# An encoder block's token mixer: the triangular inverse kept on its own chunk's lanes, one triangle merged and transposed by VectorE

## The chip, the cores and the metric

The kernel runs on one core of a Trainium2 chip. A core has a matrix engine (TensorE, "PE" in the profile, its weight loads "PEld"), VectorE ("DVE"), ScalarE ("ACT"), GpSimd ("POOL") and SyncE ("SP"), which issues most DMAs. The engines run their own instruction queues in order and meet at semaphores. The metric is the device time of one execution in microseconds. The kernel before took 3065.03 us, the median of three runs (3062.26 to 3070.91).

## The reference

One layer of a streaming encoder, 2048 tokens, width 1024, float32:

1. Token mixing: RMSNorm, one input projection, an RWKV-7 group (8 heads of 64) beside a gated spatial group, one output projection.
2. RMSNorm and cross-attention (4 heads) into 256 memory tokens.
3. RMSNorm and a SwiGLU feed-forward layer, then a last RMSNorm.

The change lies in the RWKV-7 group. Per head the reference runs this recurrence over the tokens:

```python
sa = jnp.einsum('bhvk,bhk->bhv', S, -kk_t)
S = (S * w_t[:, :, None, :]
     + sa[..., None] * (kk_t * a_t)[:, :, None, :]
     + v_t[..., None] * k_t[:, :, None, :])
y = jnp.einsum('bhvk,bhk->bhv', S, r_t)
```

The kernel computes it in chunks of 64 tokens. Within a chunk the steps depend on each other through a strictly triangular 64x64 matrix of scores, so each head and chunk needs the inverse of a unit triangular matrix.

## The kernel before

The kernel has three stages: input projections (to about 612 us of the profiled span), the mixer (about 612 to 1140 us), and the output projection, attention and feed-forward layer (the rest, which is dense matrix products). The change touches the mixer alone.

**Groups and units.** The mixer takes 16 groups of 128 tokens (`GROUPS`, `L`). A group has 8 heads, named by `m` (0 to 3) and `e` (0, 1), and two chunks of 64 tokens, `a` (0, 1): sixteen units. A head's channels lie on 64 partitions, `lane(e)`; a chunk's tokens lie on 64 partitions, `lane(a)`.

**Quarters of the array.** All matmuls of the inverse and of the state are 64x64: operands on 64 partitions, a result on 64 partitions. Each therefore uses one quarter of the array, named here by the half its operands lie on and the half its result goes to. (0 to 0) and (1 to 1) are the two diagonal quarters. A float32 matmul stands in the trace as two records.

**The inverse.** It grows by levels: blocks of 1 are joined to 2 (the "first" step), then b = 2, 4, 8, 16, 32 (`LEVELS`) are joined to 2b. At each level:

- `cross` multiplies the scores with the left blocks of the inverse (to PSUM);
- ScalarE's `evac_x` copies the product to `xm`;
- `merge` multiplies with the right blocks;
- VectorE's `take_level` puts the result into the inverse under a mask (`copy_predicated`).

The left factor must be had transposed, so `tu` holds each unit twice, as T and as its transpose U. `merge` computes both sides with two matmuls for each unit (L1911 for T, L1913 for U; at the last level U alone). U of a unit lies on the lanes `up(e, a)`, which is `a` for e = 1 and the other chunk's for e = 0. `first_pairs` makes blocks of 2 with 32 small matmuls (L1882, L1884). Every level goes in two halves, g = 0 and 1, of eight units: PE, ACT and DVE each do one half while another does the other. The inverse is used by `solve` (L1968).

**The order.** Three pipelines run beside each other in one body: state work of group k, the inverse of group k + 1 ("behind"), and the preparation of group k + 2 ("ahead"). Each engine's `body` writes its order out by hand. On PE (L1995 on): from_values, state_out 0, state_in 0, scores b, solve 0, scores k, state_add 0, chunk_out 0, first_pairs, state_out 1, state_in 1, cross 0, solve 1, merge 0, state_add 1, cross 1, chunk_out 1, loras, merge 1, key_norms, variance, turn_gate, cross 2, turn k, merge 2, turn b, cross 3, turn_v, merge 3, bonus_sums, key_scales, scale_back, cross 4, lora_g, mix_gate, merge 4. On DVE: right_sides 0, scores b (two `take`), next_state 0, first (2), right_sides 1, scores k (2), level 0, next_state 1, gate_sigmoid, level 1, sum_decays (sig, cum, k_mix), gate_stats, level 2, reciprocals, deviation, level 3, bonuses, keys_normed, normalised, queries, mixed, level 4, decayed. On ACT: identities, solved 0, loras_in, gate_in, evac 0, solved 1, evac 1, outputs, lora_tanh, evac 2, k_tok, roots, deviation, evac 3, b_tok, v_tok, exps, evac 4, gates.

Of the kernel before, what the change touches and what calls it, by code (L numbers as in the profile page):

```python
# [13 lines left out]
P = 128  # L14
# [56 lines left out]
def hybrid_block_kernel(nc, xT, memT, gains, weights, shift_mu, w_lora, a_lora, g_lora, head_cols,  # L71
                        kk_rows, lnx_rows, kk_cols, rk_spread, w_spatialT, b_spatial, sgu_ln, consts, cen,
                        head_mean, scan_reset, block_masks, tri_masks, half_ident, tri_wide, outT):
    with ExitStack() as ctx:
# [164 lines left out]
        tu = [rw(f"tu{i}", [P, 2, 2, 2, 2, C]) for i in range(2)]  # L239
# [43 lines left out]
        for n in ("const_in in_first in0 in1 in2 in3 xr_in0 xr_in1 sqa_done ws_zero const_ready mixers_done w_raw0 w_raw1 w_hi_done w_lo_done job_done job_out act_in sq_done sumsq_done "  # L283
# [7 lines left out]
                  "id_done sc_b sc_k sc_1 ev_b ev_k x_ps x_ev tu_ps tu_ev rhs_ps rhs_ev sa_ps sa_ev h_ps h_add h_new "  # L291
# [161 lines left out]
        def up(e, a):  # L453

            return a ^ 1 ^ e

        def both(t, g, b):

            first = t[:, g]
            return bass.AP(first.tensor, first.offset, [[16 * C, P], [4 * C + b, 2], [2 * b, 2 * C // b], [1, b]])  # L460

        def rights(t, g, b):
            return t[:, g, 1].rearrange("p e m (n two b) -> p (e m n) two b", two=2, b=b)[:, :, 1, :]
# [622 lines left out]
        def _(act):  # L1086
# [107 lines left out]
            def identities(n, par):  # L1194
                if n >= 2:
                    act.wait_ge(S["sa_ps"], 2 * n - 2)
                act.activation(tu[par][:].rearrange("p g u e m t -> p (g u e m) t"), half_id[:].unsqueeze(1).to_broadcast([P, 4 * HP, C]),
                               ACT.Copy).then_inc(S["id_done"], 1)
# [433 lines left out]
        def _(pe):  # L1632
# [221 lines left out]
            def scores(n, par, src, need, bank, done):  # L1854
# [3 lines left out]
                if n:  # L1858
                    pe.wait_ge(S["tu_ev"], 12 * n)
                elif bank:  # L1860
                    pe.wait_ge(S["job_out"], 2 * Q_TAIL)
# [1400 lines left out]
```

## Time and profile before

| what | value |
|---|---|
| runs, median (lowest to highest) | 3065.03 us (3062.26 to 3070.91) |
| profiled execution: span | 3061.7 us |
| share of the span that PE is busy | 97% |
| granted TensorE clock, mean over the span | 0.98 of full |
| DVE, ACT, POOL busy | 53%, 33%, 47% |
| the mixer's 15 stretches from one `from_values` to the next | 498.54 us |
| PE busy, mean granted clock in the fastest and slowest of them | 28.22 of 30.25 us at 1.00; 32.57 of 35.22 us at 0.85 |

The span runs from the first to the last instruction that the profiler recorded; the execution that was profiled has no other time of its own, and what lies around the span is seen only as the 3.3 us between it and the median of the runs. Busy time is the union of an engine's records. A PE record lasts about 0.22 us though the next one can start after 0.01 to 0.03 us, so the length of a step is read from start to start.

### The profile page before, as it was taken

The page shows a single profiled execution, that of the slowest core. Times are in us where ns is not written, and L with a number is a line of the kernel's source. Part 1 is how long each engine was busy: PE and PEld are TensorE (multiplying, and loading weights), DVE is VectorE, ACT ScalarE, POOL GpSimd, SP SyncE. Part 2 cuts the span into 40 slices and gives each one's busy share as a digit, 9 for nine tenths or more (in the row PEclk, how much of TensorE's full clock was granted, in tenths as well). Part 3 has the DMA queues.
Part 4 walks back from the last instruction along what each step waited for, and adds up shares of the span by engine and source line. Part 5 has one row for each costly group of instructions (what it writes and reads, how often), then busy time and mean ns, then how long its engine had stood idle before and what let it go on. Part 6 is the DMA issues. An engine that isn't in the chain of part 4 may idle for free.

```text
span 3061.7 us, 62501 instructions
## 1 busy us (share of the span) xinstructions
PE 2955.4 (97%) x26858; PEld 2523.8 (82%) x26858; DVE 1613.3 (53%) x2010; ACT 1001.8 (33%) x1692; POOL 1432.3 (47%) x993
## 2 busy tenths in 40 slices
PE   8999999989998989999999999999999999999998
PEld 7888888788888878998788888787898788888887
DVE  6332643365666653234866664545232876665452
ACT  4123211233443442233433332222232433332222
POOL 4555454333443445437544442446625654443344
PEclk9999999988998999999999999999999999999999
DMA  4433454321112222111223326454111123335642
GB/s 167 165 102 111 159 161 157 123 59 43 43 49 67 68 60 93 42 42 42 110 110 138 138 111 254 173 198 158 42 48 49 69 110 125 138 125 217 231 152 85
DMA packets 176012, 347.25 MB, mean 113 GB/s; under 512 B 47232, under 2 KB 104576, under 8 KB 170112
## 3 DMA queue, kind: packets, MB, share of 16 engines
q1 hardware_dynamic: 175744, 343.35, 32.5%
q8 instruction: 208, 3.41, 0.5%
q14 instruction: 60, 0.49, 0.1%
HBM read 240.53 MB, written 102.76 MB: 112 GB/s over the span
## 4 chain that ended last, share of the span: by engine, by line
PE 70%; DVE 6%; issue 2%; DMA 2%; ACT 1%; POOL 1%; SPq 0%; DVEq 0%; ACTq 0%; POOLq 0%
PE ps L2201 28%; PE ps L1641 19%; PE ps L2153 6%; PE ps L1747 2%; PE ps L1911 2%; PE ps L1913 2%; PE ps L1895 2%; PE ps L1865 1%; DMA w_raw<-in_weights 1%; DVE tu L2481 1%; DMA hidden<-hid 1%; PE ps L1992 1%; PE ps L1796 1%; PE ps L1819 1%; PE ps L1851 1%
## 5 line engine op out<-in xcount | busy, mean ns | idle before, releaser
L803 POOL TENSOR_TENSOR w_lo<-w_raw,w_hi 128x512 fp32r<-128x512 f32 x256 | 383.1, 1519 | 503.8 <-ACT w_hi L1093 500.0
L1641 PE MATMUL ps<-a_hi,w_hi 128*128 128x512 f32 x1140 | 446.3, 391 | 16.1 <-DVE a_lo L2381 9.6
L1641 PE MATMUL ps<-a_lo,w_hi 128*128 128x512 f32 x1140 | 444.4, 390 | 0.0
L1093 ACT ACTIVATE w_hi<-w_raw 128x512 fp32r<-128x512 f32 x252 | 144.8, 623 | 656.9 <-PE ps L1641 509.8
L1641 PE MATMUL ps<-a_hi,w_lo 128*128 128x512 f32 x1140 | 351.5, 390 | 0.0
L2201 PE MATMUL ps<-a_hi,w_hi 128*128 128x512 f32 x800 | 314.8, 393 | 10.3 <-ACT u_t L1462 4.9
L2201 PE MATMUL ps<-a_lo,w_hi 128*128 128x512 f32 x800 | 313.2, 391 | 0.0
L2201 PE MATMUL ps<-a_hi,w_lo 128*128 128x512 f32 x800 | 312.9, 391 | 0.0
L1641 PEld LDWEIGHTS ps<-a_hi,w_hi 128*128 128x128 f32 x1140 | 214.5, 188 | 62.9 <-DVE a_lo L2381 9.6
L1641 PEld LDWEIGHTS ps<-a_hi,w_lo 128*128 128x128 f32 x1140 | 214.3, 188 | 44.9
L1641 PEld LDWEIGHTS ps<-a_lo,w_hi 128*128 128x128 f32 x1140 | 214.5, 188 | 44.1 <-issue 0.2
L1020 POOL TENSOR_TENSOR w_lo<-w_raw,w_hi 128x512 fp32r<-128x512 f32 x100 | 139.8, 1398 | 182.6 <-ACT w_hi L1453 182.6
L1020 POOL TENSOR_TENSOR w_lo<-s,w_hi 128x512 fp32r<-128x512 f32 x100 | 143.8, 1438 | 169.5 <-ACT w_hi L1453 169.5
L2736 DVE TENSOR_TENSOR x<-ps,x 128x1024 f32 (+1 forms) x63 | 76.6, 1221 | 268.3 <-PE ps L1641 255.6
L2389 DVE TENSOR_TENSOR z_ext<-ps,rstd 128x1024 f32<-128x1024 f32 x44 | 53.9, 1225 | 305.0 <-PE ps L1641 304.5
L1641 PE MATMUL ps<-b_hi,w_hi 128*128 128x512 f32 x512 | 202.7, 396 | 3.7 <-DVE x L2736 3.7
L1641 PE MATMUL ps<-b_lo,w_hi 128*128 128x512 f32 x512 | 201.4, 393 | 0.0
L1020 POOL TENSOR_TENSOR xw_lo<-s,xw_hi 128x512 fp32r<-128x512 f32 x100 | 145.1, 1455 | 109.8 <-ACT xw_hi L1453 109.8
L2201 PE MATMUL ps<-t_hi,xw_hi 128*128 128x512 f32 x496 | 193.1, 389 | 0.2
L2201 PE MATMUL ps<-t_hi,xw_lo 128*128 128x512 f32 x496 | 193.0, 389 | 0.0
L2201 PE MATMUL ps<-t_lo,xw_hi 128*128 128x512 f32 x496 | 193.0, 389 | 0.0
L2201 PEld LDWEIGHTS ps<-a_hi,w_hi 128*128 128x128 f32 x800 | 151.2, 189 | 46.1 <-ACT u_t L1462 6.6
(369 smaller groups left out, 6658.3 us busy)
## 6 DMA issues: line engine op xcount, KB each, us to landing
w_raw<-in_weights SPq DMA_DIRECT2D x228, 512.0 KB, 4.0
hidden<-hid SPq DMA_DIRECT2D x44, 1024.0 KB, 3.9
zT<-z_out SPq DMA_DIRECT2D x44, 512.0 KB, 3.8
a_hi<-hidden SPq DMA_DIRECT2D x44, 512.0 KB, 8.2
a_lo<-hidden SPq DMA_DIRECT2D x44, 512.0 KB, 9.1
w_raw<-kvw SPq DMA_DIRECT2D x32, 512.0 KB, 3.2
suv<-zT SPq DMA_DIRECT2D x16, 512.0 KB, 5.0
x<-in_xT SPq DMA_DIRECT2D x16, 512.0 KB, 6.1
```

The lines of the kernel that those rows point to most:

```text
L803: pool.tensor_tensor(low_t[:, u, part, :], w_raw[:, u, part, :], high[:, u, part, :].bitcast(F32), ALU.subtract).then_inc(S["w_lo_done"], 1)
L1020: pool.tensor_tensor(operand(o, p)[1], operand_raw[o], operand(o, p)[0].bitcast(F32), ALU.subtract).then_inc(S["sw_lo"], 1)
L1093: act.activation(split_into(pair)[0][:, u, part, :], w_raw[:, u, part, :], ACT.Copy).then_inc(S["w_hi_done"], 1)
L1641: mm = pe.matmul(to[:, nb, 0:w], wt[:, u, k, :], r[:, k, nb * w:(nb + 1) * w], start=(k == 0 and r is hi_in and wt is w_hi), stop=(k == kn ...
L1747: mm = pe.matmul(cols(bank, m), lhs[:, m * P:(m + 1) * P], rhs[:, (m // 2) * C:(m // 2) * C + L], start=True, stop=True)
L1895: mm = pe.matmul(unit(h, 2 * g * (lv > 0) + e, 2 * L + g * C * (lv == 0) + mh * 32, 32), atrb[par][lane(a), e, 2 * mh + g, 0, :], t_u, sta ...
L1911: pe.matmul(unit(a, *t_at, 32), u_u, x_u.rearrange("p (n two b) -> p n two b", two=2, b=b)[:, :, 0, :], start=True, stop=True)
L1913: mm = pe.matmul(unit(h, 2 * g + 1, (e + 1) * C + mh * 32, 32), x_u, u_u.rearrange("p (n two b) -> p n two b", two=2, b=b)[:, :, 1, :], st ...
L2153: mm = pe.matmul(to, st[:, k, at:at + P], wt[:, 0:2, k, :], start=(k == 0 and n == 0 and t % 2 == 0), stop=(k == KT - 1 and n == 2), skip_ ...
L2201: mm = pe.matmul(to, wt[:, k, :], r[:, k, :], start=(k == 0 and n == 0 and not more), stop=(k == HT - 1 and n == 2), skip_group_check=True)
L2389: dve.tensor_tensor(z_ext[:, u, 1:TB + 1], flat(src), rstd[:], ALU.mult).then_inc(S["job_out"], 1)
L2736: dve.tensor_tensor(at_k(x, k), flat(slot(beside + u)).unsqueeze(1), at_k(x, k), ALU.add).then_inc(S["job_out"], 1)
```

## The change

The inverse of a unit stays on its own chunk's lanes, once (`inv`). Only one triangle is merged on PE. The transposed operand that `cross` needs is made by a VectorE instruction, `transpose`, over all sixteen units (512 columns), which transposes each 32x32 block into `inv_t`. `first_pairs` is gone: DVE takes the odd columns out of the scores themselves. Each level is one step for all sixteen units, on PE, ACT and DVE.

```diff
-        tu = [rw(f"tu{i}", [P, 2, 2, 2, 2, C]) for i in range(2)]
+        inv = [rw(f"inv{i}", [P, 2, HP, C]) for i in range(2)]
+        inv_t = rw("inv_t", [P, 2, HP, C])
 ...
-                if lv == 0:
-                    if n == 0:
-                        act.wait_ge(S["late_zero"], 1)
-                    act.wait_ge(S["x_ps"], 10 * n + 2)
-                    act.activation(xm[:].rearrange("p e g m (n two b) -> p e (g m n) two b", two=2, b=b)[:, :, :, 0, :],
-                                   ps[:, 0:2, 2 * L:2 * L + 2 * C].rearrange("p e (n b) -> p e n b", b=b), ACT.Copy).then_inc(S["x_ev"], 2)
-                    return
-                for g in range(2):
-                    act.wait_ge(S["x_ps"], 10 * n + 2 * lv + g + 1)
-                    act.activation(xm[:, :, g].rearrange("p e m (n two b) -> p e (m n) two b", two=2, b=b)[:, :, :, 0, :],
-                                   ps[:, 2 * g:2 * g + 2, 2 * L:2 * L + C].rearrange("p e (n b) -> p e n b", b=b), ACT.Copy
-                                   ).then_inc(S["x_ev"], 1)
+                if n == 0 and lv == 0:
+                    act.wait_ge(S["late_zero"], 1)
+                act.wait_ge(S["x_ps"], 5 * n + lv + 1)
+                act.activation(xm[:].rearrange("p e g m (n two b) -> p e (g m n) two b", two=2, b=b)[:, :, :, 0, :],
+                               ps[:, 0:2, 2 * L:2 * L + 2 * C].rearrange("p e (n b) -> p e n b", b=b), ACT.Copy).then_inc(S["x_ev"], 1)
 ...
-            def by_tile(g):
-
-                return [(mh, e, a, up(e, a)) for mh in range(2) for e in range(2) for a in range(2)]
-
-            def first_pairs(n, par):
-
-                pe.wait_ge(S["ev_b"], 2 * n + 2)
-                for g in range(2):
-                    for mh in range(2):
-                        for a in range(2):
-                            for e in range(2):
-                                m, at = 2 * mh + g, 2 * L + g * C + mh * 32
-                                q_u, b_u = qr[par][lane(e), 0, m, a, :], bt[lane(e), m, a * C:(a + 1) * C]
-                                pe.matmul(unit(a, e, at, 32), q_u,
-                                          b_u.rearrange("p (n two) -> p n two", two=2)[:, :, 0], start=True, stop=True)
-                                mm = pe.matmul(unit(up(e, a), e, L + at, 32), b_u,
-                                               q_u.rearrange("p (n two) -> p n two", two=2)[:, :, 1], start=True, stop=True)
-                mm.then_inc(S["sc_1"], 1)
+            def by_tile():
+
+                return [(m, e, a) for m in range(HP) for e in range(2) for a in range(2)]
 
             def cross(n, par, lv):
 
                 b = LEVELS[lv]
-                for g in range(2):
-                    pe.wait_ge(S["tu_ev"], 12 * n + 2 * lv + (g + 1 if lv else 2))
-                    for mh, e, a, h in by_tile(g):
-                        t_u = tu[par][lane(a), g, 0, e, mh, :].rearrange("p (n two b) -> p n two b", two=2, b=b)[:, :, 0, :]
-                        mm = pe.matmul(unit(h, 2 * g * (lv > 0) + e, 2 * L + g * C * (lv == 0) + mh * 32, 32),
-                                       atrb[par][lane(a), e, 2 * mh + g, 0, :], t_u, start=True, stop=True)
-                    mm.then_inc(S["x_ps"], 1)
+                if lv == 0:
+                    pe.wait_ge(S["ev_b"], 2 * n + 2)
+                pe.wait_ge(S["inv_tr"], 5 * n + lv + 1)
+                for m, e, a in by_tile():
+                    t_u = inv_t[lane(a), e, m, :].rearrange("p (n two b) -> p n two b", two=2, b=b)[:, :, 0, :]
+                    mm = pe.matmul(unit(a, e, 2 * L + m * 32, 32), atrb[par][lane(a), e, m, 0, :], t_u, start=True, stop=True)
+                mm.then_inc(S["x_ps"], 1)
 
             def merge(n, par, lv):
 
                 b = LEVELS[lv]
-                last = lv == len(LEVELS) - 1
-                for g in range(2):
-                    pe.wait_ge(S["x_ev"], 10 * n + 2 * lv + g + 1)
-                    if lv == 0:
-                        pe.wait_ge(S["ev_k"], 2 * n + 2)
-                    for mh, e, a, h in by_tile(g):
-                        x_u, u_u = xm[lane(h), e, g, mh, :], tu[par][lane(h), g, 1, e, mh, :]
-                        if not last:
-                            t_at = (2 * g + 1, mh * 32) if e else (2 * g, BANK - C + mh * 32)
-                            pe.matmul(unit(a, *t_at, 32), u_u,
-                                      x_u.rearrange("p (n two b) -> p n two b", two=2, b=b)[:, :, 0, :], start=True, stop=True)
-                        mm = pe.matmul(unit(h, 2 * g + 1, (e + 1) * C + mh * 32, 32), x_u,
-                                       u_u.rearrange("p (n two b) -> p n two b", two=2, b=b)[:, :, 1, :], start=True, stop=True)
-                    mm.then_inc(S["tu_ps"], 1)
 ...
                 for m, e, a in by_pair(j):
-                    mm = pe.matmul(unit(up(e, a), 4 + e, j * L + (m % 2) * C), qr[par][lane(e), 0, m, a, :], h_st[lane(e), j, m, :],
+                    mm = pe.matmul(unit(a, 4 + e, j * L + (m % 2) * C), qr[par][lane(e), 0, m, a, :], h_st[lane(e), j, m, :],
 ...
                 for m, e, a in by_pair(j):
-                    mm = pe.matmul(unit(a, 6 + e, (2 + j) * L + (m % 2) * C), tu[par][lane(up(e, a)), m % 2, 1, e, m // 2, :],
-                                   rhs_t[lane(up(e, a)), e, m % 2, :], start=False, stop=True, skip_group_check=True)
+                    mm = pe.matmul(unit(a, 6 + e, (2 + j) * L + (m % 2) * C), inv[par][lane(a), e, m, :],
 ...
+            def turned(n, par, lv):
+
+                dve.wait_ge(S["tu_ev"], 6 * n + lv + 1)
+                dve.transpose(inv_t[:].rearrange("p e m t -> p (e m) t"), inv[par][:].rearrange("p e m t -> p (e m) t")).then_inc(S["inv_tr"], 1)
 
             def take_first(n, par):
-                dve.wait_ge(S["sc_1"], n + 1)
+                dve.wait_ge(S["sc_b"], n + 1)
                 dve.wait_ge(S["id_done"], n + 1)
-                first = ps[:, 0:2, 2 * L:].rearrange("p e (u g x) -> p u g e x", u=2, g=2)
-                for g in range(2):
-                    base = tu[par][:, g]
-                    out = bass.AP(base.tensor, base.offset, [[16 * C, P], [4 * C + 1, 2], [2 * C, 2], [2, C]])
-                    take(out, low[:, 0].rearrange("p u (e x) -> p u e x", e=2), first[:, :, g], "tu_ev")
+                odd_cols = inv[par][:].rearrange("p e m (x two) -> p e m x two", two=2)[:, :, :, :, 1]
+                mask = low[:, 0, 1].rearrange("p (m x) -> p m x", m=HP).unsqueeze(1).to_broadcast([P, 2, HP, C // 2])
+                take(odd_cols, mask, ps[:, 0:2, :].rearrange("p e (m w x two) -> p e m w x two", w=2, x=C // 2, two=2)[:, :, :, 0, :, 1], "tu_ev")
+                turned(n, par, 0)
 
             def take_level(n, par, lv):
                 b = LEVELS[lv]
-                for g in range(2):
-                    dve.wait_ge(S["tu_ps"], 10 * n + 2 * lv + g + 1)
-                    new = ps[:, 2 * g:2 * g + 2, :].rearrange("p b t -> p (b t)")[:, BANK - C:BANK + 3 * C]
-                    if lv < len(LEVELS) - 1:
-                        take(both(tu[par], g, b), blocks(low[:, lv + 1], b), blocks(new.rearrange("p (u x) -> p u x", u=2), b), "tu_ev")
-                    else:
-                        take(rights(tu[par], g, b), low[:, lv + 1, 1].rearrange("p (n b) -> p n b", b=b),
-                             new[:, 2 * C:].rearrange("p (n b) -> p n b", b=b), "tu_ev")
+                dve.wait_ge(S["tu_ps"], 5 * n + lv + 1)
+                mask = low[:, lv + 1, 1].rearrange("p (x b) -> p x b", b=b).unsqueeze(1).to_broadcast([P, 2, HP * C // (2 * b), b])
+                take(rights(inv[par], b).rearrange("p (e x) b -> p e x b", e=2), mask,
+                     ps[:, 0:2, 0:HP * C // 2].rearrange("p e (x b) -> p e x b", b=b), "tu_ev")
+                if lv + 1 < len(LEVELS):
+                    turned(n, par, lv + 1)
 ...
                                        0.0, ALU.mult, ALU.add).then_inc(S["cum_done"], 1)
+
+            def mixing(n):
+                dve.wait_ge(S["sig_done"], n + 1)
```

`from_values` writes to `unit(a, ...)` in place of `unit(up(e, a), ...)` in the same way. The orders written out by hand become:

- PE: ..., scores k, state_add 0, **cross 0**, chunk_out 0, state_out 1, state_in 1, **merge 0**, solve 1, **cross 1**, state_add 1, **merge 1**, chunk_out 1, loras, **cross 2**, key_norms, variance, **merge 2**, turn_gate, turn k, **cross 3**, turn b, **merge 3**, turn_v, **cross 4**, bonus_sums, key_scales, **merge 4**, scale_back, lora_g, mix_gate.
- DVE: right_sides 0, **first + transpose**, scores b, next_state 0, scores k, right_sides 1, **level 0 + transpose**, next_state 1, **level 1 + transpose**, gate_sigmoid, sum_decays (sig, cum), **level 2 + transpose**, mixing (k_mix, four instructions), gate_stats, reciprocals, deviation, **level 3 + transpose**, bonuses, keys_normed, **level 4**, normalised, queries, mixed, decayed.
- ACT: as before, with one evacuation of 256 columns in each level and 512 in place of 1024 columns in `identities`.

## Rows read from the trace of the kernel before

**Rows 1.** The page: busy time by engine, and the chain by engine.
```profile
PE 2955.4 (97%) x26858; PEld 2523.8 (82%) x26858; DVE 1613.3 (53%) x2010; ACT 1001.8 (33%) x1692; POOL 1432.3 (47%) x993
...
PE 70%; DVE 6%; issue 2%; DMA 2%; ACT 1%; POOL 1%; SPq 0%; DVEq 0%; ACTq 0%; POOLq 0%
```

**Rows 2.** Windows by body: stretch, its length, busy us by engine, clock, DMA.
```profile
671.77:706.99 35.22, 32.57 (x940) 29.80 (x936) 21.65 (x44) 14.06 (x30) 14.72 (x14) 0.85 0.18 46
...
981.73:1013.08 31.35, 28.24 (x940) 25.55 (x936) 21.09 (x44) 14.20 (x30) 14.46 (x12) 1.00 0.27 69
...
1045.60:1075.85 30.25, 28.22 (x940) 25.63 (x937) 21.52 (x44) 14.02 (x30) 14.45 (x12) 1.00 0.29 74
...
sum 498.54, PE 450.56 PEld 411.27 DVE 313.90 ACT 206.54 POOL 209.78; mean PE 30.04 PEld 27.42 DVE 20.93 ACT 13.77 POOL 13.99
```

**Rows 3.** Groups by line, PE, fifteen bodies: records, busy, mean ns, idle before, releasers.
```profile
L1911 PE MATMUL ps<-xm,tu 64*64 64x32 f32 x1920 | 98.2, 232 | 2.3 <-DVE qkrm L2481 2.0
L1895 PE MATMUL ps<-tu,atrb 64*64 64x32 f32 x2400 | 63.2, 233 | 13.6 <-DVE tu L2481 8.1 <-issue 4.8
...
L1882 PE MATMUL ps<-bt,qr 64*64 64x32 f32 x480 | 18.5, 219 | 9.1 <-issue 9.1
...
L1992 PE MATMUL ps<-atrb,sa_t 64*64 64x64 f32 x480 | 16.8, 249 | 1.1 <-issue 1.1
```

**Rows 4.** Windows inside one body, cut where the granted clock changes.
```profile
810.85:822.20 11.35, 8.45 (x399) 7.76 (x396) 7.02 (x14) 2.20 (x6) 5.50 (x6) 1.00 0.37 90
822.30:829.00 6.70, 6.55 (x141) 6.19 (x137) 2.29 (x5) 1.64 (x4) 0.00 (x0) 0.50 0.31 85
```

**Rows 5.** Timeline of PE: start us, length us, line, output<-inputs, records.
```profile
1048.11 0.41 PE L1968 MATMUL ps<-rhs_t,tu 64*64 64x64 f32 x16
1048.34 0.41 PE L1974 MATMUL ps<-v_tok,k_tok 64*64 64x64 f32 x16
...
1064.04 0.66 PE L1840 MATMUL ps<-cst,kt 128*128 128x128 f32 x4
...
1066.18 0.66 PE L1840 MATMUL ps<-cst,bt 128*128 128x128 f32 x4
...
1072.40 0.67 PE L1895 MATMUL ps<-tu,atrb 64*64 64x32 f32 x32
1073.00 1.16 PE L1747 MATMUL ps<-gd,gl 128*128 128x128 f32 x8
...
1075.11 0.95 PE L1913 MATMUL ps<-tu,xm 64*64 64x32 f32 x26
1075.85 0.27 PE L1928 MATMUL ps<-v_tok,qkrm 64*64 64x64 f32 x2
```

**Rows 6.** Timeline of DVE, same columns.
```profile
1048.35 1.38 DVE L2481 COPY_PREDICATED atrb<-tri,ps 128x512 f32<-128x512 uint8 x2 [0.65 <-PE ps L1865]
...
1051.85 1.30 DVE L2481 COPY_PREDICATED tu<-low,ps 128x256 f32<-128x256 uint8 x2 [0.60 <-PE ps L1884]
...
1061.69 0.43 DVE L2481 COPY_PREDICATED tu<-low,ps 128x256 f32<-128x256 uint8 x1 [2.90 <-PE ps L1913]
...
1062.74 0.68 DVE L2537 TENSOR_SCALAR sig<-th 128x1024 f32<-128x1024 f32 x1
1063.45 1.23 DVE L2541 TENSOR_TENSOR_SCAN cum<-reset,sig 128x512 f32<-128x512 f32 x1
...
1068.18 0.71 DVE L2568 TENSOR_SCALAR v_hat<-ps,bn 128x512 f32<-128x512 f32 x1
```

**Rows 7.** Timeline of ACT, same columns.
```profile
1048.59 0.38 ACT L1240 ACTIVATE sa_t<-ps 128x256 f32<-128x256 f32 x1 [3.11 <-PE ps L1968]
...
1054.62 0.40 ACT L1174 ACTIVATE xm<-ps 128x256 f32<-128x256 f32 x1 [4.63 <-PE ps L1895]
...
1060.83 1.02 ACT L1204 ACTIVATE th<-ps 128x1024 f32<-128x1024 f32 x1 [1.07 <-PE ps L1747]
...
1067.00 0.36 ACT L1216 ACTIVATE n<-ps,eps 128x128 f32<-128x128 f32 x1
```

More of the change, by code:

```diff
@@ L290, in hybrid_block_kernel @@
                   "lg_ps gate_done bon_ps bon_v bonus_done vtr ktr btr vtc ktc btc "
-                  "id_done sc_b sc_k sc_1 ev_b ev_k x_ps x_ev tu_ps tu_ev rhs_ps rhs_ev sa_ps sa_ev h_ps h_add h_new "
+                  "id_done sc_b sc_k inv_tr ev_b ev_k x_ps x_ev tu_ps tu_ev rhs_ps rhs_ev sa_ps sa_ev h_ps h_add h_new "
                   "qkv_ps y0_ps y_ps yc_cp yc_sq yv_ps yv_rt yv_rc yb_ps yn_done yb_done yo_done y_st met_pe met_dve met_sp").split():
@@ L451, in side, with rights @@
             return j ^ (m // 2)
[L453 to L463, printed above, removed]
+        def rights(t, b):
+            return t[:].rearrange("p e m (n two b) -> p (e m n) two b", two=2, b=b)[:, :, 1, :]
         def bank4(b):
@@ L1917, in from_values @@
+                pe.wait_ge(S["x_ev"], 5 * n + lv + 1)
+                for m, e, a in by_tile():
+                    u_u = inv[par][lane(a), e, m, :].rearrange("p (n two b) -> p n two b", two=2, b=b)[:, :, 1, :]
+                    mm = pe.matmul(unit(a, e, m * 32, 32), xm[lane(a), e, m // 2, m % 2, :], u_u, start=True, stop=True)
+                mm.then_inc(S["tu_ps"], 1)
             def from_values(k, par):
@@ L1927, in from_values @@
                     for m, e, a in by_pair(j):
-                        mm = pe.matmul(unit(up(e, a), 4 + e, j * L + (m % 2) * C), qkrm[par][lane(a), e, m, 0, :], v_tok[par][lane(a), m, e, :],
+                        mm = pe.matmul(unit(a, 4 + e, j * L + (m % 2) * C), qkrm[par][lane(a), e, m, 0, :], v_tok[par][lane(a), m, e, :],
                                        start=(j == 0 and m % 2 == 0), stop=True, skip_group_check=True)
@@ L2009, in body @@
                     state_add(k, par, 0)
+                if behind:
+                    cross(b, q, 0)
+                if state:
                     chunk_out(k, par, 0)
-                if behind:
-                    first_pairs(b, q)
-                if state:
                     state_out(k, par, 1)
@@ L2016, in body @@
                 if behind:
-                    cross(b, q, 0)
+                    merge(b, q, 0)
                 if state:
@@ L2020, in body @@
                 if behind:
-                    merge(b, q, 0)
+                    cross(b, q, 1)
                 if state:
@@ L2024, in body @@
                 if behind:
-                    cross(b, q, 1)
+                    merge(b, q, 1)
                 if state:
@@ L2030, in body @@
                 if behind:
-                    merge(b, q, 1)
+                    cross(b, q, 2)
                 if ahead:
@@ L2035, in body @@
                     variance(k)
+                if behind:
+                    merge(b, q, 2)
                 if ahead:
@@ L2038, in body @@
                 if behind:
-                    cross(b, q, 2)
                     turn(b, kt, "kt_done", 4, ahead, "ktr")
-                    merge(b, q, 2)
+                    cross(b, q, 3)
                     turn(b, bt, "bt_done", 5, ahead, "btr")
-                    cross(b, q, 3)
+                    merge(b, q, 3)
                     turn_v(b, q, ahead, state)
-                    merge(b, q, 3)
+                    cross(b, q, 4)
                     bonus_sums(b, q)
@@ L2048, in body @@
                     key_scales(n)
+                if behind:
+                    merge(b, q, 4)
                 if state:
@@ L2051, in body @@
                 if behind:
-                    cross(b, q, 4)
                     lora_g(b, q)
@@ L2055, in body @@
                     mix_gate(n, state)
-                if behind:
-                    merge(b, q, 4)
             for pair in range(Q_IN1, Q_TAIL):
@@ L2623, in body @@
                 if scores:
+                    take_first(b, q)
                     take_scores(b, atrb[q], 0, "sc_b", "ev_b")
@@ L2636, in body @@
                 if scores:
+                    take_level(b, q, 1)
                     gate_sigmoid(b, q)
-                    take_level(b, q, 1)
                 if ahead:
                     sum_decays(n)
-                    gate_stats(n)
                 if scores:
@@ L2644, in body @@
                 if ahead:
+                    mixing(n)
+                    gate_stats(n)
                     reciprocals(n)
@@ L2652, in body @@
                     keys_normed(n, state)
+                if scores:
+                    take_level(b, q, 4)
                 if state:
@@ L2657, in body @@
                     mixed(n)
-                if scores:
-                    take_level(b, q, 4)
-                if ahead:
                     decayed(n)
@@ L2681, in _ @@
                         sum_decays(0)
+                        mixing(0)
                         gate_stats(0)
```

14 lines of the change are left out of this document (6 added, 8 removed).

## The prediction

> **What bounds the kernel now.** I read the page first. PE is busy for 97% of the span, and the chain that ended last runs 70% on PE, with DVE far behind at 6% [rows 1]. So a change pays only if PE gets through sooner. The change touches the mixer, so the next view is the windows cut by body, from one `from_values` to the next. Fifteen of them last 498.54 us, 33.2 each; PE is busy for 30.0 of that, DVE for 20.9, ACT for 13.8 and POOL for 14.0 [rows 2]. Of the bodies run wholly at full clock (three: 31.35 to 30.25 us) the mean is 31.4. The reader is to see that PE has only about 3 us of idle time in a body. The groups by line say whose it is: eleven groups lose 35.2 us together to "issue", from 9.1 (L1882) down to 1.1 (L1992), with no engine named, 2.3 us a body; `cross` (L1895) loses 8.1 to DVE's `tu` [rows 3]. The last view is the windows inside a body: its sparse part (PE busy for 8.45 of 11.35 us) is followed by 6.7 us at a granted clock of 0.50, which is 1.2 GHz [rows 4]. PE had idled before the fall.
>
> **What a 64x64 step costs PE.** The timeline at full clock gives four. `cross` 4 puts 32 records on all four quarters, 8 on each, and the next step starts 0.60 us later. Merge 4 has 32 records on the two diagonal quarters only, and its first 26 (13 a quarter) span 0.95. `solve`, 16 records on four quarters, gives way after 0.23. Merge 2 fills the time between the transposes of kt and bt, 2.14 us less the 0.58 of the first: 1.56 [rows 5]. One rule fits all: a record holds its quarter for 0.058 us, and the fullest quarter sets the step. Cross 4: 8 x 0.058 = 0.47, plus 0.13 of handing over. The 26 records: 12 x 0.058 + the record's own 0.22 = 0.92 (0.95 read). Solve: 4 x 0.058 = 0.23. Merge 2: 64 records, but T for e = 0 alone leaves the diagonal, so each diagonal quarter holds 24: 1.40 + 0.16.
>
> **The change on PE, per body.** It keeps every unit on its own lanes, so cross, merge, from_values and solve now use the diagonal quarters alone.
> - first_pairs goes: 16 records a quarter, -0.93.
> - Four merges go from 24 to 16 on the fullest quarter: 4 x -0.47 = -1.87. Merge 4 stays at 16.
> - Five crosses go from 8 to 16: 5 x +0.47 = +2.33.
> - Two solves go from 4 to 8: 2 x +0.23 = +0.47. from_values goes from 8 to 16: at most +0.47; today it starts behind merge 4's quarters, so I take half, +0.24.
>
> Sum +0.24 us. 192 records of 940 leave each body and PE gains nothing.
>
> The Trainium skill speaks otherwise in one place: "TensorE: Matmul & The Clock Gate", Part 3 (The mechanism), says that a weight load overlaps matmuls in flight only when the row group differs. By that the new order, which alternates the two row halves, would run as fast as cross today. The trace does not settle it, since merge 4's order is 1, 0, 0, 1, but its 0.95 us is nearer to the quarter rule; the other case is a rival below.
>
> **The change on the chain.** Today the halves g = 0 and 1 cover each other. Afterwards each level is one string: cross, evacuation, merge, take, transpose, cross. Prices: ACT 0.40 for 256 columns (L1174) [rows 7]; DVE's masked copy of 256 columns 0.43, but 1.30 for two where it writes runs of one or two elements (first, level 0), which overlap by 0.1, so about 0.74 for one that is waited for; the score copies 1.38 for two [rows 6]; from PE's last start to a reader 0.30 (solve 1048.34, `sa_t` 1048.59), back to PE 0.05 [rows 5, 7]. DVE `transpose` stands nowhere in the trace. Lower bound 0.40: `sig` does 1024 columns in 0.68, half is 0.34 and a start. Upper bound 1.3: the scan needs 1.23 for 512. `v_hat` needs 0.71 for 512 [rows 6]; I take 0.70, the row of the same size. By the skill's "VectorE: DVE Perf Modes" (The three transpose paths: 311 ns for 128x128 bf16; Specifications: 0.96 GHz) an estimate would be 0.31 + 384/0.96 ns = 0.71.
>
> Walking the new order once at full clock, PE will wait at the places below; where I write 0.1 it is two hand-overs of 0.05.
> 1. Cross 0, for `ev_b`: 0.30 + first 0.74 + transpose 0.70 + two score copies 1.39 = 3.1 after scores b; over it lie solve 0.47, the token products 0.23, scores k 0.88, state_add 0.23. Wait 1.3. Behind it are queued chunk_out 0 and state_out 1, so the state recurrence waits too.
> 2. state_out 1, for chunk_out 0's own end (first_pairs covered it): 0.3.
> 3. Cross 1: 0.30 + 0.74 + 0.70 + 0.1 = 1.8, less solve and products 0.70: 1.1.
> 4. Merge 1: 0.30 + 0.40 + 0.05 less state_add 0.23: 0.5.
> 5. Merge 2: 0.75 less norms and variance 0.56: 0.2 (`lora_tanh`'s 1.02 on ACT [rows 7] is as long as the cross).
> 6. Cross 3: 0.30 + 0.43 + 0.70 + 0.1 less two steps of 0.60: 0.4 (sig and cum, 1.9 on DVE [rows 6], delay level 2 a little).
> 7. Merge 3: evac 3 stands on ACT behind the root of gate_stats, and gate_stats now on DVE behind level 2, its transpose and k_mix. From cross 3's start: 1.0 + 0.6 + 0.15 on DVE, two roots 0.6, evacuation 0.4 = 2.75; over it cross 3 1.06 and turn b 0.60. Wait 1.1.
> 8. Cross 4, behind three reciprocals, v_hat and level 3 with its transpose: 3.7 after the root, less 0.7 + merge 3 1.06 + turn_v 1.10: 0.9.
> 9. Merge 4, behind exps: 0.2.
>
> Together 6.0 us. The k_mix delay of 0.4 us for POOL costs nothing: POOL's string ends before the next body's scores b need it.
>
> **The sum.** The fastest body is 30.25 long, PE idle for 2.0 of it [rows 2], and at each of its five waits a record's end of 0.22 counts as busy though no step needs it: 30.25 - 2.0 - 1.1 = 27.1 of steps. With 31.4 for a body at full clock that leaves 4.3 for waits and issue. Afterwards: 27.1 + 0.24 + 6.0 + issue. Issue idles fall where 64x64 records come thickest, in the first part of a body: 399 in 11.35 us [rows 4]; that part loses first_pairs' 64 and merge 0's 32 and becomes longer. I take 2.3 -> 0.5 (bounds 0 and 2.3). New body 33.8, so +2.4 at equal clock. Fourteen such bodies give +34; the first and last, with parts missing, +2 together (the first has less work to lay over the string, the last has DVE and ACT freed). ACT's identities halves from 1024 columns, off the path. SP's queue and DMAs are untouched. 3061.7 + 36 = 3098 of span; the median of the runs lies 3.3 above the span, so **3101 us**. Nothing outside the mixer moves.
>
> **Rivals.**
> - *Diagonal quarters at row-group speed.* Cross stays at 0.47, merges fall to it: PE work -5.1 us in place of +0.24, of which half turns into longer waits because PE laid that work over the string (body about 30.7 + 0.5). Against 31.4 that is -0.2 a body, 3062; with a 0.4 us transpose -1.0 a body, about 3050, and this is the case that ends faster. It decides at a cross step under 0.7 us. Against it: merge 4's 0.95. Chance 0.15 (0.09 of it faster, 0.06 near no change).
> - *The clock.* PE idles longer and oftener, and today a fall follows the sparse part [rows 4]. Half as much again of the 6.7 us at 1.2 GHz in each body, 3.4, costs up to 1.7: 14 x 1.7 = 24, giving 3125. Against it: bodies as sparse kept 1.00 [rows 2]. Chance 0.25.
> - *A slow transpose.* At 1.3 us, +0.6 at each of five; where it lies open +2.2 a body: 3132. Chance 0.08.
> - *The walk overstates waits.* If in-order idle overlaps the issue idle as it does today, +1.0 a body remains: 3079 (3070 to 3085). Chance 0.12, a third of it within no change.
>
> Forecast as summed: 0.40. Over 0.3% is what a measurement of this kernel can tell from no change, so the bounds are 3056 and 3074. Faster 0.11, same 0.14, slower 0.75. The range 3052 to 3138 leaves out the far end of the first rival and a slow transpose at a low clock.
>
> **What would show it.** Right: L1895 with 32 records takes about 0.95 us from start to next step, merges the same; PE busy in a body unchanged near 28 at full clock though its records fall to 748; PE idle named by `inv_t` and `xm`, 5 to 6 us; "issue" under 1 us. Wrong: cross steps of 0.6; transposes of 0.4 or over 1; PE idle still mostly "issue"; full-clock bodies under 32 us. The forecast fails on its sign if full-clock bodies stay under 31.4.

## The result and the profile after

The changed kernel takes 3097.79 us (median of 4 runs, 3095.98 to 3107.98), the kernel before 3064.24 (median of 4): ratio 1.0099, 95% interval 1.0068 to 1.0131. It is slower, and 3 us under the 3101 forecast. The profiled spans are 3061.7 and 3094.2 us.

The page after: busy time by engine, and the first line of the chain that ended last.
```profile
PE 2952.9 (95%) x23786; PEld 2519.3 (81%) x23786; DVE 1628.2 (53%) x1994; ACT 984.1 (32%) x1628; POOL 1433.3 (46%) x993
...
PE 16%; DMA 2%; DVE 1%; ACT 0%; SPq 0%; issue 0%; POOL 0%; DVEq 0%; ACTq 0%
```
3072 records of PE are gone [rows 1], 192 in each of the sixteen bodies as counted, and PE is busy for only 2.5 us less. The chain is no help here: followed back from the end it now breaks off before it comes to the mixer. So I read windows.

Windows of the kernel after (stretch, length, busy us by engine, granted clock, DMA share, GB/s): two bodies at full clock, and all fifteen.
```profile
1006.27:1040.74 34.47, 28.42 (x743) 25.63 (x741) 23.05 (x41) 13.09 (x27) 14.17 (x12) 1.00 0.24 62
1040.74:1074.20 33.46, 27.95 (x743) 25.41 (x741) 22.14 (x41) 13.05 (x26) 14.52 (x12) 1.00 0.25 64
649.41:1172.52 523.11, 444.47 (x11051) 402.58 (x11049) 328.47 (x601) 190.71 (x381) 208.30 (x173) 0.94 0.19 51
```
A body's window has 743 records in place of 940 (by their starts 740 and 932, which is the 192; a window also counts those that reach into it), but PE is busy for the same 28 us of it [rows 2]. Over the full-clock bodies (three before, seven after, the shorter last body left out) the means are 28.31 busy and 3.07 idle before, 28.30 busy and 5.66 idle after: 31.37 and 33.95 us. The three before are 30.25, 31.36 and 32.52 us long, so their mean is known to about a microsecond only. All that a body became longer is idle time of PE.

Groups by line of PE after, the fifteen bodies (records, busy, mean ns, idle before them, what ended it).
```profile
L1876 PE MATMUL ps<-inv,xm 64*64 64x32 f32 x2400 | 88.5, 225 | 18.9 <-ACT xm L1166 17.2 <-issue 1.6
L1867 PE MATMUL ps<-inv_t,atrb 64*64 64x32 f32 x2400 | 87.5, 224 | 44.3 <-DVE inv_t L2455 31.0 <-DVE atrb L2443 12.9
```
Against [rows 3] the picture has turned round: cross waits 44.3 us in place of 13.6, and "issue" (PE idle though it waits for nothing that the profile shows), which had 36.1 us of 48.0 over all PE groups before, has 4.8 of 78.6 after.

The timeline of PE after, in the body from 1006.27 (start, length, line, output<-inputs, records, idle before and its releaser).
```profile
1027.34 1.12 PE L1867 MATMUL ps<-inv_t,atrb 64*64 64x32 f32 x32 [0.26 <-DVE inv_t L2455]
1028.40 0.66 PE L1826 MATMUL ps<-cst,bt 128*128 128x128 f32 x4
1030.07 1.12 PE L1876 MATMUL ps<-inv,xm 64*64 64x32 f32 x32 [1.02 <-ACT xm L1166]
1031.12 1.16 PE L1837 MATMUL ps<-cent,zin 128*128 128x128 f32 x8
1033.28 1.12 PE L1867 MATMUL ps<-inv_t,atrb 64*64 64x32 f32 x32 [1.00 <-DVE inv_t L2455]
...
1039.71 1.09 PE L1815 MATMUL ps<-ws,v_lnb 128*64 128x128 f32 x16 [0.79 <-DVE y_n L2579]
```
A cross now holds PE for 1.06 us from its start to the next step's (1027.34 to 1028.40), against 0.60 in [rows 5]; a merge for 1.05. In order the rows are cross 3, the turn of bt, merge 3, turn_v, cross 4 and, last, `mix_gate`, which waits for y_n.

The timeline of DVE in the same body.
```profile
1009.96 0.74 DVE L2443 COPY_PREDICATED inv<-low,ps 128x256 f32<-128x256 uint8 x1 [0.89 <-PE ps L1851]
1010.73 0.71 DVE L2455 STREAM_TRANSPOSE inv_t<-inv 128x512 f32<-128x512 f32 x1
1011.37 1.29 DVE L2443 COPY_PREDICATED atrb<-tri,ps 128x512 f32<-128x512 uint8 x2
...
1038.56 0.44 DVE L2443 COPY_PREDICATED inv<-low,ps 128x256 f32<-128x256 uint8 x1
1038.89 0.68 DVE L2579 TENSOR_TENSOR y_n<-y_cen,ps 128x512 f32<-128x512 f32 x1
```
The transpose takes 0.71 us. The last two rows, with the last of PE's above, show what I had not seen coming: y_n stands behind the copy of level 4, and the gate's matmuls on PE wait for it.

### The profile page after: what moved, and what is told of

Same layout as the page of the kernel before. It is cut to its first block and busy times, and to the rows that moved or that the text cites. A ratio compares the mean times of both kernels' runs of the same rounds, so it can differ in the third digit from the quotient of the medians.

```text
span 3094.2 us, 56260 instructions
## 1 busy us (share of the span) xinstructions
PE 2952.9 (95%) x23786; PEld 2519.3 (81%) x23786; DVE 1628.2 (53%) x1994; ACT 984.1 (32%) x1628; POOL 1433.3 (46%) x993
```

## The experiments

**How the times are compared.** Executions of one kernel differ by up to 43 us (the kernel before, 3053.22 to 3096.21), and with them the mean granted clock: the changed kernel took 3086.28 us at 0.985 and 3108.72 at 0.977. Inside each kernel the two lie on a line; over 124 executions of eleven kernels its common slope is 2.24 us (+-0.17) per 0.001 of clock. "At equal clock" below is each kernel's mean brought to 0.980 with it: my working, beside the measured medians. The +- is the 95% interval of that mean from the kernel's own executions; with four of them it is wide. The slopes of single kernels lie between 1.65 and 3.09, and the line takes the clock for something that comes from outside, though part of it is the kernel's own doing (see below). So I read the result beside the trace. The last three columns are means over the full-clock bodies of the trace, without the last body; bodies of one kernel differ by up to 2.3 us, and some kernels have three such bodies or none. The 49 executions of the kernel before were made beside the experiments; the four of the result are not among them.

| kernel | median us (runs) | clock | at equal clock | full-clock body | PE busy in it | idle |
|---|---|---|---|---|---|---|
| before | 3069.6 (49) | 0.980 | 3069.2 +-1.1 | 31.37 | 28.31 | 3.07 |
| after, e5_after_again | 3097.8 (8) | 0.980 | 3099.3 +-1.5 | 33.95 | 28.30 | 5.66 |
| e1_before_diag_cross | 3081.9 (10) | 0.982 | 3088.0 +-1.2 | 33.10 | 30.47 | 2.63 |
| e2_quarters | 3090.3 (10) | 0.975 | 3079.6 +-2.0 | 33.42 | 26.22 | 7.19 |
| e3_no_transpose | 3098.9 (4) | 0.973 | 3080.4 +-7.9 | 33.75 | 28.56 | 5.19 |
| e4_order | 3059.7 (10) | 0.983 | 3068.6 +-2.0 | 31.38 | 28.08 | 3.30 |
| e6_gate_only | 3103.2 (4) | 0.974 | 3086.9 +-5.5 | none | - | - |
| e7_before_fewer_t | 3044.2 (9) | 0.982 | 3048.7 +-2.4 | 30.72 | 26.96 | 3.77 |
| e8_order2, e11 | 3022.7 (9) | 0.987 | 3038.2 +-1.2 | 29.65 | 28.08 | 1.56 |
| e9_fill | 3077.8 (7) | 0.991 | 3104.4 +-1.0 | 34.04 | 29.53 | 4.51 |
| e10_order2_fill | 3017.5 (4) | 0.991 | 3042.7 +-3.7 | 29.69 | 28.07 | 1.62 |

**The quarter rule, in both kernels and both directions.** In the kernel before:
```diff
-  mm = pe.matmul(unit(h, 2 * g * (lv > 0) + e, ...   # cross
+  mm = pe.matmul(unit(a, 2 * g * (lv > 0) + e, ...
```


> The kernel before, with one change: the cross matmuls of the inverse write their results to the lanes that they read from, so that they use the two diagonal quarters of TensorE in place of all four (the products land on other units' lanes than the reference's; counts, sizes and waits are those of before). Quarter rule (each record holds its quarter for 0.058 us, the fullest quarter sets the step): a cross of one half, 32 records, goes from 8 to 16 records a quarter, its step from 0.60 to about 1.05 us; over five levels up to +2.3 us of PE a body, some of it hidden in issue idle that is there today, so +1.4 to +2.3 a body, in sixteen bodies +20 to +36 us: about 3084 to 3100 in all. Rival (only a change of row group matters, diagonal quarters run as fast as four): cross step stays at 0.60, total within 0.3% of before.

In the changed kernel:
```diff
-  mm = pe.matmul(unit(a, e, 2 * L + m * 32, 32), ...   # cross
+  mm = pe.matmul(unit(a ^ 1 ^ e, e, 2 * L + m * 32, 32), ...
```


> The changed kernel, with one thing different: the cross matmuls write to the other chunk's lanes for half of their records, so that all four quarters of TensorE are used (the products land on other units' lanes than the reference's; counts, sizes and waits are the changed kernel's). Quarter rule: the cross step falls from 1.05 to 0.60 us, but the string cross, evacuation, merge, copy, transpose goes on as long as before behind it, so only part of the 5 x 0.45 is gained, about 0.9 us a body and 14 us in all: 3084, between 3075 and 3090. Rival (row groups): no change of the step, 3098.

One full-clock body of each, first e1, then e2 (windows, columns as above), and two steps of e2 (timeline of PE).
```profile
1060.77:1094.42 33.65, 30.49 (x940) 28.02 (x937) 22.80 (x44) 14.16 (x30) 14.41 (x12) 1.00 0.26 66
```
```profile
890.50:924.17 33.67, 26.49 (x742) 23.51 (x740) 22.98 (x41) 13.09 (x27) 14.30 (x14) 1.00 0.22 55
```
```profile
911.09 0.67 PE L1867 MATMUL ps<-inv_t,atrb 64*64 64x32 f32 x32 [0.64 <-DVE inv_t L2455]
913.77 1.12 PE L1876 MATMUL ps<-inv,xm 64*64 64x32 f32 x32 [1.42 <-ACT xm L1166]
```
The same records cost +2.16 us of PE a body on two quarters in place of four, and -2.08 the other way; by the rule it is 2.33. The cross of e2 lasts 0.67 in place of 1.12. The row-group rival would have had both at nothing and is refuted: which quarters a step loads sets its time. The totals say less than the steps: e1 is slower than before by 0.48% (interval 0.13 to 0.82) or 18.8 us at equal clock, a little under the range expected (its median, 3081.85, too). e2 is 19.7 us (+-2.3) below the changed kernel at equal clock, where 14 were expected, but its clock is lower, its median falls by only 7.5 us, to the edge of the range, and its three full-clock bodies are only 0.53 us shorter (0.9 expected). What the quarters are worth in the step is shown, what they are worth in the total lies between 8 and 20 us.

**The transpose.**
```diff
-  pe.wait_ge(S["inv_tr"], 5 * n + lv + 1)
+  pe.wait_ge(S["tu_ev"], 6 * n + lv + 1)      # and cross reads inv; no dve.transpose
```


> The changed kernel without VectorE's five transposes of the merged inverse per body: cross reads the merged inverse itself and waits for the copy that wrote it (so the computation leaves the transposition out). If the string of each level is what PE waits for, the 0.71 us goes from the places where it stands open (cross 0, 1, 3, 4, partly refilled by other waits): about 1.4 us a body, 20 us in all, 3078, between 3068 and 3085. Rival (PE's own work is the bound and the transposes lie beside it): within 0.3% of the changed kernel, 3098. If the transposes alone were the loss, it would return to 3064 or below.

At equal clock 18.9 us go, but with four executions that is +-8, and the trace shows less: its execution had the clock of the changed kernel's (0.982) and a span 12.7 us shorter, 9.2 of them in the fifteen bodies (513.9 against 523.1, with 58.4 and 58.7 us at half clock). The median does not move (3098.92), outside the range expected; the executions ran at clocks from 0.967 to 0.982. So the transposes cost something like 10 to 20 us here, and no run fixes it closer. PE's idle time in the fifteen bodies falls from 78.6 to 68.0 only: waits for the inverse go from 31.2 to 13.9 and for `atrb` from 12.9 to 3.4, but `xm` (17.3 to 22.2) and issue (4.8 to 11.9) come up in their place. Even with no transpose at all the kernel stays about 11 us (+-8) above the one before at equal clock: it is one part of the string, not the cause by itself.

**The order of the work.** Nothing is left out in any of these. The order of e4:
```diff
-ACT  k_tok, roots (with root_gate), deviation, evac_x 3
+ACT  k_tok, roots, evac_x 3, root_gate, deviation
-DVE  deviation, take 3, bonuses, keys_normed, take 4, normalised
+DVE  take 3, deviation, bonuses, keys_normed, normalised, take 4
-PE   cross 0, chunk_out 0 ... cross 1, state_add 1, merge 1, chunk_out 1 ... merge 4, scale_back
+PE   chunk_out 0, cross 0 ... state_add 1, cross 1, chunk_out 1, merge 1 ... scale_back, merge 4
```


> The changed kernel with the same work in another order, nothing left out. ACT: the evacuation of cross 3 goes ahead of the roots of gate_stats. VectorE: the take of level 3 goes ahead of gate_stats' deviation part, that of level 4 behind normalised (mix_gate waits 0.58 us a body for it today). PE: chunk_out 0 ahead of cross 0, state_add 1 ahead of cross 1, chunk_out 1 ahead of merge 1, scale_back ahead of merge 4. If the loss of the change is waits in the string and not PE's work, 2.5 to 3.4 us of them go from a body: full-clock bodies of about 31 in place of 34.0, 3055 to 3065 in all, level with the kernel before or a little below. Rival (the waits only move, since the string of five levels is as long as what can be laid over it): at most 1 us a body, 3083 to 3098. A third: what was hidden by them becomes late elsewhere (the state recurrence or the gates), over 3098.

And one part of it alone:
```diff
-DVE  take 4, normalised
+DVE  normalised, take 4
-PE   merge 4, scale_back
+PE   scale_back, merge 4
```


> The changed kernel, nothing left out, with one part of the reordering alone: scale_back ahead of merge 4 on PE, normalised ahead of the take of level 4 on VectorE. It takes away the wait of mix_gate for y_n, 8.7 us in fifteen bodies, that the prediction did not list. If each wait counts by itself: 0.4 to 0.6 us a body, 6 to 9 us in all at an equal clock, 3087 to 3091. Rival (the time comes back at the next body's scores b or at level 4, since the same string follows): no change within 3 us.

Groups by line of e4, the fifteen bodies; they answer to the two rows of after above.
```profile
L1882 PE MATMUL ps<-inv,xm 64*64 64x32 f32 x2400 | 89.9, 226 | 9.2 <-ACT xm L1166 5.4 <-issue 3.7
L1873 PE MATMUL ps<-inv_t,atrb 64*64 64x32 f32 x2400 | 88.7, 225 | 26.1 <-DVE inv_t L2461 17.1 <-DVE atrb L2449 6.4 <-issue 0.9
```
The waits of the two groups fall from 63.2 to 35.3 us, a full-clock body from 33.95 to 31.38 with about the same PE work (28.30 and 28.08). That is the whole loss of the change, undone by order alone: 3059.66 us, ratio 0.9971 to the kernel before (0.9929 to 1.0013, not told apart from it), and at equal clock 0.6 us (+-2.2) from it. e6 takes away the one wait that the prediction missed. It goes (8.7 us for y_n, now none; idle in all 78.6 to 65.1), and at equal clock 12.4 us go (+-5), which holds the 6 to 9 expected; but the median is 3103.22, over the range. The clock was at 0.974.

**The other side of the change by itself**: the kernel before with fewer T merges.
```diff
-  if not last:
+  if lv == 0:
       pe.matmul(unit(a, *t_at, 32), u_u, ...
```


> The kernel before with the merge matmuls of T left out in levels 1 to 3 (only the U side is merged there; level 0 still merges both; VectorE's copies and all waits stay, so the T that cross reads is old). 96 of 940 records a body go, all from the diagonal quarters. Quarter rule and issue supply together: each of three merges goes from 24 to 16 records on its fullest quarter, 3 x 0.47 = 1.4 us a body, and some of the 2.3 us of issue idle goes as well; 21 to 33 us in all at an equal clock, 3031 to 3045. Rival (VectorE's takes or PE's other steps would be late in their place): under 10 us.

PE busy falls by 1.35 us a body (1.4 expected), the ratio is 0.9922 (0.9901 to 0.9942), at equal clock -20.5 us (+-2.5), just under what was expected: issue idle falls from 36.1 to 29.4, but waits for `tu` rise from 8.8 to 15.4 and for `bt` from 0.5 to 5.6. So the removal of T was worth having; what the change paid for it, on PE, was five crosses on two quarters.

**The order taken further.**
```diff
-PE   turn kt, cross 3, turn bt, merge 3, turn_v, cross 4, bonus_sums, key_scales
+PE   turn kt, turn bt, cross 3, turn_v, merge 3, bonus_sums, cross 4, key_scales
+PE   cross 0: the 16 records of e = 0 once their copy is done, then those of e = 1
-ACT  evac_x 2, k_tok, roots, evac_x 3, root_gate, deviation
+ACT  evac_x 2, roots, deviation, k_tok, evac_x 3, root_gate
-DVE  mixing, gate_stats, key reciprocal, v_hat, take 3 ... queries, mixed, decayed
+DVE  gate_stats, mixing, v_hat, take 3, key reciprocal ... decayed, mixed, queries
```


> The order of the run e4_order, nothing left out, and these as well. PE: the turn of bt ahead of cross 3, turn_v ahead of merge 3, bonus_sums ahead of cross 4; cross 0 begins with the units of e = 0 once their scores are copied. ACT: the roots of the key norms and of the deviation ahead of the copy of k_tok. VectorE: gate_stats ahead of mixing; the reciprocal of the key norms behind the take of level 3; decayed, mixed, queries in place of queries, mixed, decayed. Of the 3.1 us of waits in a full-clock body of e4_order (scores b 0.49, cross 0 0.57, sa_t 0.26, cross 1 0.13, cross 3 0.47, merge 3 0.37, cross 4 0.84) about 2.0 go: full-clock bodies of 29.4 in place of 31.4, 30 us less in all, 3025 to 3040, and faster than both kernels. Rival (the string of five levels, three times 1.5 and twice 0.75 us between the steps, is then itself what the body lasts, or VectorE with its 23 us busy becomes late): 3045 to 3060.

Windows of e8: one body, the last body, and all fifteen.
```profile
971.04:1001.09 30.05, 28.21 (x743) 25.86 (x741) 23.11 (x42) 13.17 (x27) 14.20 (x12) 1.00 0.28 71
1060.20:1100.47 40.27, 34.56 (x690) 31.76 (x689) 15.63 (x28) 8.42 (x18) 9.72 (x8) 0.66 0.16 54
645.01:1100.47 455.46, 427.35 (x11050) 392.18 (x11049) 339.82 (x601) 192.77 (x382) 207.34 (x176) 0.97 0.23 59
```
3022.66 us, ratio 0.9843 (0.9813 to 0.9873): faster than both. Fourteen bodies last 29.2 to 30.2 us (29.4 expected) with PE idle for 1.6. The rival, a string that no order can cover, is refuted. One thing was off, in its favour: its clock is 0.987, so that it is a little better than the range (at equal clock, 3038.2, it lies inside). And its last body, with less work in it, runs for 27 of its 40.3 us at half clock, which is what the mean of 0.66 in its row says; the stretch of 30.7 us that the text on e10 names goes on behind the body. What such an order would give the kernel before, which idles for 3.07 us a body, I have not tried.

**What brings the clock down.** Kernels e2, e3 and e6 gained 12 to 20 us at equal clock and gave most or all of it back in a lower clock (for e2 and e6 clear of the spread; e3's four executions are too few for that); e8 gained both ways. In the trace before, all 11 falls in the fifteen bodies begin 7.6 to 14.6 us into a body, in the sparse part [rows 4]. In the two traces of the changed kernel 9 of 16 begin at 22.5 to 25.5, a place where none began before. One of them (windows of the kernel after):
```profile
968.71:991.40 22.69, 19.08 (x590) 17.54 (x588) 15.95 (x32) 8.06 (x18) 5.27 (x5) 1.00 0.35 91
991.40:1005.05 13.65, 13.62 (x136) 12.53 (x136) 5.47 (x10) 3.87 (x7) 8.20 (x7) 0.50 0.00 0
```
The granted clock is 1.00 in the first row and 0.50, which is 1.2 GHz, in the second. PE is busy through the whole of the slow stretch; it had idled ahead of it, for 0.47 us at cross 3 and 0.97 at merge 3. All nine begin like this, in the last 0.1 us of merge 3's wait or up to 1.5 us behind it, and ahead of the wait of cross 4. So I filled the wait of merge 3, and that of cross 4 with it:
```diff
+  def fill(n):                              # ahead of merge 3, and ahead of cross 4
+      pe.wait_ge(S["ev_k"], 2 * n + 2)
+      for i in range(6):
+          pe.transpose(cols(2 + i % 2, i // 2), ident, ident)
```


> The changed kernel again, unchanged, on the chip that runs the three others of this set, so that they have it beside them and so that its time can be read against the granted clock of many executions. 3092 to 3106; at a mean granted clock of 0.982 about 3096.

> The changed kernel, nothing left out, with idle transposes of the identity put on PE ahead of merge 3 and ahead of cross 4: six each, 0.7 us each, into two banks that nothing reads then. They lie in waits of 1.02 and 1.00 us, so the steps start when they did. In the traces of the changed kernel 9 of 16 falls of the granted clock begin at 22.5 to 25.5 us of a body, behind these waits. If the falls there come from PE's idle time: hardly any fall begins there, the mean granted clock goes from 0.980 to 0.986 or more, and the time to 3080 to 3090, while at an equal clock it stays. Rival (the falls have another cause, or more work on PE brings more of them): falls at the same place, clock within 0.002 of the changed kernel's, 3096 to 3106.

Windows of e9, the fifteen bodies.
```profile
644.30:1155.35 511.05, 443.01 (x11230) 401.86 (x11229) 335.90 (x601) 191.21 (x382) 208.41 (x175) 0.99 0.20 52
```
No fall begins at that place, there are two in all (at 13.2 and 18.4), and half-clock time in the fifteen bodies goes from 58.7 and 92.2 us in the two traces of the changed kernel to 10.2. Work that computes nothing makes the kernel 20 us faster: 3077.81 (3075.35 to 3083.47) against 3086.28 to 3108.72, a little more than expected. A full-clock body is no shorter (34.04), and at equal clock the kernel is 5 us slower (+-1.6), where I had expected no change: so the gain is the clock alone, less those 5 us. Another chip is not behind it, since the kernel before kept its clock there (mean of ten executions 0.980). That the falls at this place go when the waits before them are filled is shown. Elsewhere the changed kernel had 7 falls in thirty bodies and e9 has 2 in fifteen, too few to tell. The changed kernel's own repetition (e5) was spread wider than expected, 3086.28 to 3108.72. Why e2 (with more idle time than the changed kernel), e3 and e6 (with less) had a lower clock than it, is not shown: I can't name from the rows what tells a body that falls from one that doesn't.

And the same in the further order, in the first and the last body only:
```diff
+  if not state:  fill(4, 6)    # ahead of cross 0; 4 ahead of merge 0, 8 ahead of cross 1, 5 ahead of merge 1
+  if not ahead:  fill(2, 14)   # in place of loras; 6 in place of turn_gate
```


> The order of e8_order2, nothing left out, with idle transposes of the identity on PE in the first and the last body alone, where parts of the work are missing (23 in the first, 0.12 us each, in the waits of levels 0 and 1; 20 in the last in place of loras and turn_gate). In the trace of e8_order2 the granted clock is at half for 30.7 us of the last body, which lasts 40.3 us in place of 29.5, and the first lasts 36.0. If idle time lets the clock fall there: the last body under 36 us, the first under 34, together 5 to 12 us less, 3011 to 3018. Rival (fill delays the string where the wait is shorter than it, and the clock falls all the same): 3022 to 3030.

> The kernel of e8_order2 again, unchanged, beside e10_order2_fill on the same chip: 3008 to 3030, median about 3022, mean granted clock 0.985 to 0.993.

The last body of e10 takes 31.3 us in place of 40.3 and 40.4 in the two traces without fill, the first 33.9 in place of 36.0 and 41.8. The median is 3017.53 (3013.63 to 3021.41), that of e8 and e11 together 3022.66 (3008.11 to 3035.74). The places answered as expected; e11 came out higher than expected (median 3025.53, up to 3035.74, clock 0.981 to 0.989), the totals overlap, and the ratios to the kernel before (0.9844 and 0.9866, intervals of +-0.003) don't separate the two.

## Why the prediction was right, step by step

- **The quarter rule and the PE sum.** +0.24 us a body was forecast, and PE's busy time, which also holds the ends of records before waits, changed by -0.01 (28.31 to 28.30). Its largest terms hold each for itself: crosses +2.33 forecast, +2.16 and 2.08 in e1 and e2; merges -0.47 a level, -0.45 in e7 (1.35 for three). The Trainium skill's row-group rule ("TensorE: Matmul & The Clock Gate", Part 3, The mechanism), that a load overlaps matmuls in flight only when the row group differs, names a condition; my rival took it for the only one. It is not what sets the step here: units alternate row halves in both cases, and 32 records take 1.05 us on two quarters and 0.60 on four.
- **The transpose.** 0.70 taken, 0.71 measured.
- **The nine waits.** 6.0 us forecast. In the body from 1006.27, forecast and measured: cross 0 1.3, 1.02; state_out 1 0.3, 0.10; cross 1 1.1, 0.85; merge 1 0.5, 0.22; merge 2 0.2, 0; cross 3 0.4, 0.26; merge 3 1.1, 1.02; cross 4 0.9, 1.00; merge 4 0.2, 0. These make 4.5 us of idle time. Another 1.5 stood where I had listed none: mix_gate for y_n 0.79 (8.7 us in the fifteen bodies), scores b for bt 0.67 (only 1.2 in the fifteen). But idle time isn't what I had summed: my waits run from the point where the step before would have handed over, while the trace counts the end of its last record as busy. For cross 0, state_add starts at 1011.22 and hands over 0.23 later, and the cross starts at 1012.72: 1.27 us, against 1.3 forecast and 1.02 of idle time. Read so, the nine make about 5.5 us and the two overlooked ones 1.7, and with the 27.3 us of steps that the forecast had (27.1 + 0.24) they give this body's 34.47. So the single waits were priced well, 0.5 too high in all; the two that were overlooked are what the forecast lacked. In this body, the longest of the seven, they made it 0.6 too short (33.8). In the mean of the seven it is off by 0.15 only, since the wait for bt is nearly absent there: that is in part luck. The one of mix_gate was in the diff to be read, since normalised stands behind the take of level 4 and scale_back behind merge 4.
- **Issue idle.** 2.3 to 0.5 a body forecast, 2.4 to 0.3 measured (36.1 and 4.8 us in fifteen). That it falls where records go was right, but the number of records alone doesn't set it: with all 940 it is 36.1 on four quarters and 28.4 with the crosses on two (e1), with 844 it is 29.4 (e7), and with 743 it lies between 4.8 and 11.9 (the changed kernel, e2, e3, e4). What sets it is open.
- **The body.** 33.8 us at full clock forecast, 33.95 measured; +2.4 and +2.6. The prediction gives the three full-clock bodies before as 31.35 to 30.25; the longest is 32.52 (1013.08 to 1045.60), and the mean of 31.4 holds it.
- **The total.** +36 forecast, +30 at equal clock, +32.5 between the profiled spans. The way there is not quite the forecast one. The fifteen bodies give +24.5 (498.6 to 523.1), since their half-clock time fell from 75.1 to 58.7 us (in the second trace of the changed kernel it is 92.2, and they give +37.1); the first body gives +9.1 (31.3 to 40.4), where I had at most +2, because 30 of its 40 us ran at half clock, against 10. "Equal clock" was the weak step: it holds for the mean (0.980 in both kernels, 8 and 49 runs), and for neither part. The 3.3 us that I laid on the span hold 1.8 around it, in every run of the result, and 1.5 by which the profiled execution lay below the median.
- **The rivals.** Row-group speed: refuted by e1 and e2. The clock: right about the mechanism (new waits, a new place for falls) and wrong about the balance, since the old falls in the sparse part became rarer. Slow transpose: no (0.71). Overstated waits: no, the full-clock bodies grew by 2.6 us and not by 1.0.

## What to carry to other kernels

Count 64x64 records by the quarter that they load, and let the fullest quarter set the step: records moved onto it were paid almost in full here (2.16 of 2.33 us), and records taken off it came back (1.35 of 1.4). By the same count records taken off the other quarters shorten no step; no run takes away those alone. When two halves that covered each other are joined into one string, list every step that stands behind the string in the queues of the other engines too, and then write the order anew: here the order was worth 75 us between the medians and 61 at equal clock, twice what the change cost (30). How much of that the kernel before could have had by a new order too was not measured. Where PE must wait about a microsecond a few times in a body, look at where the granted clock falls next, and count work laid into the wait as possibly worth more than nothing.

## What I had not expected of the hardware

- Idle transposes, 12 a body, raised the mean granted clock from 0.980 to 0.991 and took 20 us off.
- The mean clock of an execution explains most of the spread between executions of one kernel (85% of its variance): 2.24 us per 0.001, and a standard deviation of 1 to 5 us left.
- Removing a wait can cost as much in clock as it saves: e6 took 13.5 us of idle time out of fifteen bodies, ran at a clock of 0.974 in place of 0.980, and was no faster.
